# Two linear attentions in a decoder kernel: VectorE's masked copies moved behind the next level's logarithms, and sixteen small sums spread over the first products of an inverse

## Chip, cores and metric

The kernel runs on one core of a Trainium2 chip. What counts is the time of one execution in microseconds (us), as the device measures it; the median of three is given. Lower is better.

## What is computed

The reference is two blocks in a row over one sequence of 512 tokens of width 1024: two hybrid attention and retention layers, then a block of feed-forward, token mixer and feed-forward. Only the token mixer matters here. It has a pooling branch, two gated linear attentions ("hgrn" and "gla") and an RWKV-7 recurrence, all fed from one projection and joined by one output projection:

```python
p = (u @ w_in).astype(jnp.float32)
o_h = chunked_gated_linear_attention(silu(hq) * QK_SCALE, 1.0 - f, hi, log_f)      # "hgrn"
o_g = chunked_gated_linear_attention(gq * QK_SCALE, gk, gv, log_a)                 # "gla"
# both: S_t = diag(a_t) S_{t-1} + k_t^T v_t,  o_t = q_t S_t
o_r = rwkv7_scan(r_h, decay, k_h, v_h, kk, a)
# S_t = S_{t-1} diag(w_t) - (S_{t-1} kk_t)(kk_t * a_t)^T + v_t k_t^T ;  o_t = S_t r_t
bonus = jnp.sum(r_h * k_h * rwkv_r_k, axis=-1, keepdims=True) * v_h
y = jnp.concatenate([y_pool, y_hgrn, (gn(o_r) + bonus) * g_r, y_gla], axis=-1)
return y @ w_out
```

## The kernel before

Everything is float32. A weight matrix comes from memory in units of 128x1024 numbers. ScalarE rounds a unit to its high part (`sb_w_high`), VectorE takes the rest (`sb_w_low<-sb_raw,sb_w_high`), and TensorE makes a product of 128x512 in three passes for each of eight slices, so one unit is 24 matmuls ("a projection" below). There are three slots for split units and four for raw ones; the function `use()` on ScalarE and VectorE splits the unit three places ahead. Every engine runs its own hand-written list in order, and semaphores tie them together. A PSUM bank is taken by TensorE in turn (`take`, eight banks, those in `held` left out), and TensorE waits there until the engine that empties the bank has done so.

A linear attention (`linear_attention`, one function on each of the three engines) goes through nine levels, `ORDER = (32, 16, 8, 4, 2, 1, 64, 128, 256)`. For level n VectorE takes differences of summed logarithms (`sb_E<-sb_c_hgrn` or `sb_c_gla`, signal "log factor"), ScalarE raises them (`sb_E<-sb_E`, "exp factor"), VectorE multiplies by keys and queries (`sb_E<-sb_E,sb_kq_...`, "factors"), TensorE multiplies left by right halves ("pairs", line 789), and for levels up to 64 VectorE copies the result under a mask into `sb_near` (COPY_PREDICATED, line 1513, "pairs taken"). The buffer of the factors is double (`E2`), so the logarithms of level n+1 wait until TensorE has read level n-1 ("factors read"). Between the levels stands other work, by `fill(n)` on all three engines: `values` units, projections of the next branch, and in gla the eight tiles of the RWKV projection. VectorE lands such a tile in `sb_shifted` ("rwkv landed"), ScalarE makes `sb_mixed` of it ("rwkv own"), and VectorE adds the neighbour's share ("rwkv mixed"); before, both VectorE instructions stand together. Ahead of the levels are the "near" products (`bank<-sb_kq_hgrn`), whose four banks in hgrn were last those of the pooling outputs, emptied by ScalarE (`sb_y_pool<-bank`).

After gla's sixth level `operand_steps` prepares the RWKV operands: tanh and squares on ScalarE, small products on TensorE, a key norm (VectorE "key floored", GpSimd's power, ScalarE "key spread"), running sums, exponentials. `keep_busy(n)` gives TensorE n matmuls that nobody reads. Then `inverse` makes, for each of four heads, two triangular products AT and X (64 rows) and turns the operands of one tile with 128x128 transposes; VectorE masks the products, ScalarE lands the transposes. The "bonus" is 16 sums of two columns each, which ScalarE takes to `sb_small`, and GpSimd reads late in `inverse`.

## Time and profile before

| | before |
|---|---|
| median of 3 runs | 1789.72 us (1788.41 to 1791.04) |
| the profiled execution: its time, its span | 1789.85 us, 1788.0 us |
| busy: TensorE, VectorE, ScalarE, GpSimd | 96%, 49%, 38%, 7% of the span |
| mixer, up to the inverse's first products | about 969 to 1220 us |
| mean granted TensorE clock | 0.976 of full |

The span is what the profiler saw between the first and last instruction; 1.85 us lie around it. Times inside the profile count from the span's start. "Busy" of TensorE includes modelled pipeline ends. PEclk in a view of stretches is the granted clock: 1.00 is 2.4 GHz and 0.50 is 1.2 GHz. In a timeline row the first number is the start, the second the length, and brackets give the idle time before it with what ended it.

### The profile page before, as it was taken

To read this page: it belongs to the slowest core of one execution; us is meant where nothing else is said; L and a number is where in the kernel's file an instruction comes from. 1 tells how busy PE (TensorE), PEld (TensorE's weight loads), DVE (VectorE), ACT (ScalarE), POOL (GpSimd) and SP (SyncE) were. 2 spreads that over 40 slices of the span, in tenths; PEclk is the share of its full clock that TensorE was granted. 3 is DMA by queue.
4 is the path that set the end of the run, shared out by engine and by line. 5 is a ranking of instruction groups with operands and counts; after the bars stand their busy time and mean duration, and the time that the engine had idled before them with its cause. 6 is when DMAs were issued, how large, how long until landed. Compare 5 with 4: busy or idle time off the path is not lost.

```text
span 1788.0 us, 22298 instructions
## 1 busy us (share of the span) xinstructions
PE 1719.0 (96%) x8770; PEld 1397.2 (78%) x8770; DVE 876.0 (49%) x1169; ACT 674.9 (38%) x1017; POOL 128.8 (7%) x126
## 2 busy tenths in 40 slices
PE   7999999999999899999999999979998899999997
PEld 6777778878778788888888777858986688888886
DVE  5633445632445565444334775665345654444333
ACT  5145664225555333333223543363131433333221
POOL 0001002001000100000003100001320200000000
PEclk9999999999999999999999999977999999999998
DMA  5322213322222132333333211100001223323331
GB/s 193 122 71 71 83 49 105 122 81 82 77 66 81 53 112 97 96 104 89 98 97 130 71 60 59 51 27 1 1 19 48 83 83 100 101 95 96 93 98 56
DMA packets 40745, 143.92 MB, mean 80 GB/s; under 512 B 4816, under 2 KB 4832, under 8 KB 40384
## 3 DMA queue, kind: packets, MB, share of 16 engines
q1 hardware_dynamic: 37008, 130.87, 22.9%
q0 software_dynamic: 2192, 8.73, 1.5%
q10 hardware_dynamic: 1440, 2.88, 0.5%
q8 instruction: 70, 1.15, 0.3%
q14 instruction: 35, 0.29, 0.1%
HBM read 140.37 MB, written 2.10 MB: 80 GB/s over the span
## 4 chain that ended last, share of the span: by engine, by line
PE 79%; DVE 14%; ACT 6%; issue 1%; DMA 0%; DVEq 0%; ACTq 0%; SPq 0%
PE bank L450 22%; PE bank L452 21%; PE bank L451 21%; PE bank L432 8%; DVE sb_w_low L1126 3%; DVE sb_E L1126 2%; PE bank L438 2%; DVE sb_near L1513 1%; PE bank L668 1%; PE bank L647 1%; ACT sb_E L1844 1%; PE bank L604 1%; ACT sb_w_high L1844 1%; DVE sb_xg_low L1134 1%; DVE sb_x L1126 1%
## 5 line engine op out<-in xcount | busy, mean ns | idle before, releaser
L1126 DVE TENSOR_TENSOR sb_w_low<-sb_raw,sb_w_high 128x1024 fp32r<-128x1024 f32 (+1 forms) x253 | 310.5, 1227 | 390.4 <-ACT sb_w_high L1844 384.5
L450 PE MATMUL bank<-sb_xg_high,sb_w_high 128*128 128x512 f32 x1176 | 469.6, 399 | 25.1 <-DVE sb_xg_low L1134 15.3
L452 PE MATMUL bank<-sb_xg_high,sb_w_low 128*128 128x512 f32 x1176 | 462.0, 393 | 0.0
L451 PE MATMUL bank<-sb_xg_low,sb_w_high 128*128 128x512 f32 x1176 | 461.7, 393 | 0.0
L1844 ACT ACTIVATE sb_w_high<-sb_raw 128x1024 fp32r<-128x1024 f32 (+1 forms) x253 | 263.2, 1040 | 355.7 <-PE bank L452 325.2
L450 PEld LDWEIGHTS bank<-sb_xg_high,sb_w_high 128*128 128x128 f32 x1176 | 223.1, 190 | 92.6 <-issue 32.7
L452 PEld LDWEIGHTS bank<-sb_xg_high,sb_w_low 128*128 128x128 f32 x1176 | 223.0, 190 | 47.7
L451 PEld LDWEIGHTS bank<-sb_xg_low,sb_w_high 128*128 128x128 f32 x1176 | 223.4, 190 | 44.8
L452 PE MATMUL bank<-sb_h_high,sb_w_low 128*128 128x512 f32 x352 | 136.9, 389 | 0.0
L450 PE MATMUL bank<-sb_h_high,sb_w_high 128*128 128x512 f32 x352 | 136.9, 389 | 0.0
L451 PE MATMUL bank<-sb_h_low,sb_w_high 128*128 128x512 f32 x352 | 136.9, 389 | 0.0
L2413 POOL TENSOR_TENSOR sb_square_sum<-sb_square_sum,sb_square 128x512 f32<-128x512 f32 x34 | 44.7, 1315 | 957.7 <-ACT sb_square L1844 882.0
L450 PE MATMUL bank<-sb_w_high,sb_xg_high 128*128 128x512 f32 x256 | 103.4, 404 | 0.2 <-DVE sb_w_low L1126 0.2
L451 PE MATMUL bank<-sb_w_low,sb_xg_high 128*128 128x512 f32 x256 | 100.3, 392 | 0.0
L452 PE MATMUL bank<-sb_w_high,sb_xg_low 128*128 128x512 f32 x256 | 100.0, 390 | 0.0
L450 PEld LDWEIGHTS bank<-sb_h_high,sb_w_high 128*128 128x128 f32 x352 | 66.1, 188 | 13.8
L451 PEld LDWEIGHTS bank<-sb_h_low,sb_w_high 128*128 128x128 f32 x352 | 66.1, 188 | 13.7
L452 PEld LDWEIGHTS bank<-sb_h_high,sb_w_low 128*128 128x128 f32 x352 | 66.1, 188 | 13.6
L1844 ACT ACTIVATE sb_h_high<-sb_up 128x512 fp32r<-128x512 f32 x44 | 27.8, 632 | 118.7 <-DVE sb_up L1126 118.7
L1126 DVE TENSOR_TENSOR sb_up<-bank,sb_inv_rms 128x512 f32<-128x512 f32 x44 | 30.4, 691 | 81.5 <-PE bank L452 80.8
L1844 ACT ACTIVATE sb_gate<-sb_gate 128x512 f32<-128x512 f32 x44 | 27.8, 632 | 94.8 <-DVE sb_gate L1126 94.8
L450 PEld LDWEIGHTS bank<-sb_w_high,sb_xg_high 128*128 128x128 f32 x256 | 48.3, 189 | 18.3 <-issue 7.8
(336 smaller groups left out, 2109.0 us busy)
## 6 DMA issues: line engine op xcount, KB each, us to landing
sb_raw<-w_ffn_in SPq DMA_DIRECT2D x88, 512.0 KB, 3.3
sb_raw<-w_ffn_out SPq DMA_DIRECT2D x32, 512.0 KB, 3.5
sb_raw<-w_tok SPq DMA_DIRECT2D x24, 512.0 KB, 3.9
sb_raw<-w_mix_f SPq DMA_DIRECT2D x18, 512.0 KB, 3.2
sb_raw<-w_rot SPq DMA_DIRECT2D x16, 512.0 KB, 3.6
sb_raw<-w_qk SPq DMA_DIRECT2D x16, 512.0 KB, 3.3
sb_raw<-w_out SPq DMA_DIRECT2D x16, 512.0 KB, 3.3
sb_raw<-w_ffn_out SPq DMA_DIRECT2D x16, 384.0 KB, 3.1
```

The costliest lines, as they stand in the source:

```text
L432: made = e.matmul(out, lhsT, rhs, start=n == 0, stop=n == len(pairs) - 1)
L438: made = e.transpose(banks[i][:, blk(n)], in_, mem.ident)
L450: e.matmul(out, w[0], v[0], start=first, stop=False)
L451: e.matmul(out, w[0], v[1], start=False, stop=False)
L452: return e.matmul(out, w[1], v[0], start=False, stop=last)
L604: made = e.matmul(out[k], m.feat["rk"][r, f, blk(j)], m.feat["rq"][r, f, j * P:], start=part == 0, stop=part == 1)
L647: e.matmul(out[k], m.qT[r, j, blk(q)], m.kT[r, j, 0:keys], start=True, stop=True).then_inc(*p.up("scores", n, 2 * j + k, q))
L668: made = e.matmul(out[64 * k:64 * k + 64, blk(q)], m.tok["av"][:, key, h * ATT_DIM:(h + 1) * ATT_DIM], m.probT[:, 2 * (q % 2) + k, blk(key ...
L1126: e.tensor_tensor(out, a, b, op).then_inc(*v.up(*signal))
L1134: e.scalar_tensor_tensor(out=out, in0=a, scalar=scalar, in1=b, op0=op0, op1=op1).then_inc(*v.up(*signal))
L1844: e.activation(out, in_, func, bias=bias, scale=scale, accum_out=accum).then_inc(*a.up(*signal))
L2413: e.tensor_tensor(out, a, b, op).then_inc(*g.up(*signal))
```

## The change

VectorE's list changes most. The old `factor(n)` is cut in `logs(n)` and `factors(n)`. The masked copies of level n-1 stand between the two of level n+1; before, the copies of level n stood behind `fill(n+1)`. The logarithms of level 0 now stand before `fill(0)` and the near masks. In gla the mixing of a landed RWKV tile is cut off its landing and stands at the start of the next step (`mix`), except for tiles 2 and 5, which share a step with another. ScalarE does `factor(0)` before `fill(0)`. The bonus sums leave `operand_steps`; TensorE makes them in four pieces, two instructions each, behind the AT and X products of heads 0 and 1, and the turns of each tile come one head later. ScalarE's copy of the bonus stands behind the last landed transpose, and GpSimd waits for it.

```diff
-            yield
-            i = take(("bonus",), ("bonus",))
-            p.wait_ge(*of("rE"))
-            for t in range(TT):
-                for f in range(2):
...
+        bonus = take(("bonus",), ("bonus",))
+        held.add(bonus)
         for h in HEADS:
             gram("AT", h, m.bI, m.kkE)
+            if h < 2:
+                bonus_sums(2 * h)
             gram("X", h, m.kkE, m.bI)
-            turn_operands(h)
+            if h < 2:
+                bonus_sums(2 * h + 1)
+            if h:
+                turn_operands(h - 1)
+        turn_operands(3)
...
-            fill(0)
-            for h in HEADS:
-                v.wait_ge(*of("near product", name, h))
...
+                elif name == "gla":
+                    v.wait_ge(*of("factors read", "hgrn", len(ORDER) - 1 - n))
...
+            logs(0)
+            fill(0)
+            factors(0)
+            for h in HEADS:
+                v.wait_ge(*of("near product", name, h))
...
-            factor(0)
+
             for n in range(len(ORDER)):
+                mix(n)
                 if n + 1 < len(ORDER):
-                    factor(n + 1)
+                    logs(n + 1)
+                if n:
+                    scores(n - 1)
+                if n + 1 < len(ORDER):
+                    factors(n + 1)
                     fill(n + 1)
-                scores(n)
             v.mark("near done", name)
             fill(len(ORDER))
+            mix(len(ORDER))
...
                 tt(shifted, bank("rwkv", f)[:, :], mem.inv_rms, ALU.mult, "rwkv landed", f)
+                yield
                 v.wait_ge(*of("rwkv own", f))
...
+        def mix_gla(n):
+            if n < 6:
+                next(projections)
...
         def linear_attention(name, fill):
             q2, k2, c2, v2 = m.operands[name]
-            fill(0)
...
             factor(0)
+            fill(0)
...
-            a.wait_ge(*of("bonus in"))
-            act(small[:, 112:128], bank("bonus")[:, 0:16], "bonus")
...
+        a.wait_ge(*of("bonus in"))
+        act(mem.small[:, 112:128], bank("bonus")[:, 0:16], "bonus")
         finish_gla()
```

ScalarE's list at the start of hgrn, before (`sb_E` and `sb_c_hgrn` are the logarithms, `sb_w_high` a weight unit, `sb_y_pool` the pooling outputs):

```order
L1844 ACTIVATE sb_c_hgrn_131<-sb_c_hgrn_131 128x1024 [waits ScalarE_step]
L1844 ACTIVATE sb_w_high_51<-sb_raw_50 128x1024 [waits hgrn_logs,weights_used,weights_0]
L1844 ACTIVATE sb_w_high_51<-sb_raw_50 128x1024 [waits weights_high,weights_used,weights_1]
L1844 ACTIVATE sb_y_pool_125<-bank,sb_small_60,sb_cols_53 64x512 [waits weights_high,pool_out,pool_shift]
L1844 ACTIVATE sb_y_pool_125<-bank,sb_small_60,sb_cols_53 64x512 [waits y_pool,pool_out] x3
L1844 ACT_TABLE_LOAD [waits y_pool]
L1844 ACTIVATE sb_E_136<-sb_E_136 128x1024 [waits log_factor]
```

The same place of ScalarE in the changed kernel:

```order
L1872 ACTIVATE sb_c_hgrn_131<-sb_c_hgrn_131 128x1024 [waits ScalarE_step]
L1872 ACT_TABLE_LOAD [waits hgrn_logs]
L1872 ACTIVATE sb_E_136<-sb_E_136 128x1024 [waits log_factor]
L1872 ACTIVATE sb_w_high_51<-sb_raw_50 128x1024 [waits exp_factor,weights_used,weights_0]
L1872 ACTIVATE sb_w_high_51<-sb_raw_50 128x1024 [waits weights_high,weights_used,weights_1]
L1872 ACTIVATE sb_y_pool_125<-bank,sb_small_60,sb_cols_53 64x512 [waits weights_high,pool_out,pool_shift]
```

The table load and the exponential of level 0, which waits for VectorE's logarithms, moved ahead of the two weight units and of the pooling outputs.

VectorE's list late in gla, before, from the landing of RWKV tile 6 to the factors of level 6 (`sb_shifted` is a landed tile, `128x128x4` and `128x256x2` the shapes of levels 3 and 4):

```order
L1126 TENSOR_TENSOR sb_shifted_148<-bank,sb_inv_rms_58 128x512
L1134 SCALAR_TENSOR_TENSOR sb_mixed_147<-sb_shifted_148,sb_cols_53,sb_mixed_147 128x511
L1513 COPY_PREDICATED sb_near_138<-sb_mixer_120,bank 128x128x4 x2
L1126 TENSOR_TENSOR sb_E_137<-sb_c_gla_134 128x512 x2
L1126 TENSOR_TENSOR sb_E_137<-sb_E_137,sb_kq_gla_133 128x1024
L1126 TENSOR_TENSOR sb_w_low_52<-sb_raw_50,sb_w_high_51 128x768
L1126 TENSOR_TENSOR sb_shifted_148<-bank,sb_inv_rms_58 128x512
L1134 SCALAR_TENSOR_TENSOR sb_mixed_147<-sb_shifted_148,sb_cols_53,sb_mixed_147 128x511
L1513 COPY_PREDICATED sb_near_138<-sb_mixer_120,bank 128x256x2 x2
L1126 TENSOR_TENSOR sb_E_136<-sb_c_gla_134 128x8x64
L1126 TENSOR_TENSOR sb_E_136<-sb_E_136,sb_kq_gla_133 128x1024
```

The same stretch of VectorE in the changed kernel:

```order
L1133 TENSOR_TENSOR sb_shifted_148<-bank,sb_inv_rms_58 128x512
L1141 SCALAR_TENSOR_TENSOR sb_mixed_147<-sb_shifted_148,sb_cols_53,sb_mixed_147 128x511
L1133 TENSOR_TENSOR sb_E_137<-sb_c_gla_134 128x512 x2
L1531 COPY_PREDICATED sb_near_138<-sb_mixer_120,bank 128x128x4 x2
L1133 TENSOR_TENSOR sb_E_137<-sb_E_137,sb_kq_gla_133 128x1024
L1133 TENSOR_TENSOR sb_w_low_52<-sb_raw_50,sb_w_high_51 128x768
L1133 TENSOR_TENSOR sb_shifted_148<-bank,sb_inv_rms_58 128x512
L1141 SCALAR_TENSOR_TENSOR sb_mixed_147<-sb_shifted_148,sb_cols_53,sb_mixed_147 128x511
L1133 TENSOR_TENSOR sb_E_136<-sb_c_gla_134 128x8x64
L1531 COPY_PREDICATED sb_near_138<-sb_mixer_120,bank 128x256x2 x2
L1133 TENSOR_TENSOR sb_E_136<-sb_E_136,sb_kq_gla_133 128x1024
```

Each pair of masked copies went from ahead of the logarithms to between the logarithms and the product that waits for the exponential.

TensorE's list at the start of the inverse, as one piece of the difference (line 432 with `sb_kkE,sb_bI` is AT, with `sb_bI,sb_kkE` is X, with `sb_mixer,sb_sigma` the bonus sums; line 438 the turns, line 750 `keep_busy`):

```order
 L750 MATMUL bank<-sb_inv_rms_58,sb_ones_55 128x512 x5
-L432 MATMUL bank<-sb_mixer_120,sb_sigma_155 128x2 x8
 L432 MATMUL bank<-sb_kkE_149,sb_bI_151 128x128 x4
+L432 MATMUL bank<-sb_mixer_120,sb_sigma_155 128x2 x2
 L432 MATMUL bank<-sb_bI_151,sb_kkE_149 128x128 x4
+L432 MATMUL bank<-sb_mixer_120,sb_sigma_155 128x2 x2
+L432 MATMUL bank<-sb_kkE_149,sb_bI_151 128x128 x4
+L432 MATMUL bank<-sb_mixer_120,sb_sigma_155 128x2 x2
+L432 MATMUL bank<-sb_bI_151,sb_kkE_149 128x128 x4
+L432 MATMUL bank<-sb_mixer_120,sb_sigma_155 128x2 x2
 L438 MATMUL bank<-sb_shared_54,sb_kkE_149 128x128 x2
```

The sums, which stood in one block, are now pairs behind the first four triangular products. A row of the order is one instruction of the program; the trace shows each of these float32 matmuls as two.

## Rows read from the trace of the kernel before

**Rows 1.** The page, chain that ended last by engine.

```profile
PE 79%; DVE 14%; ACT 6%; issue 1%; DMA 0%; DVEq 0%; ACTq 0%; SPq 0%
```

**Rows 2.** Waits of TensorE from 1000 to 1250: total us, times, longest.

```profile
PE bank L432 <- ACT sb_mixed L1844: 8.7, 2, 5.4
PE bank L789 <- DVE sb_E L1126: 4.2, 2, 3.4
PE bank L450 <- ACT sb_v_hgrn L1844: 1.7, 1, 1.7
PE bank L432 <- DVE sb_ga L1126: 0.6, 1, 0.6
```

**Rows 3.** Timeline of ScalarE at the start of hgrn.

```profile
1002.73 2.23 ACT L1844 ACTIVATE sb_w_high<-sb_raw 128x1024 fp32r<-128x1024 f32 x2
1005.08 3.37 ACT L1844 ACTIVATE sb_y_pool<-bank,sb_small,sb_cols 64x512 f32<-64x512 f32 x4
```

**Rows 4.** Timeline of TensorE there: near products, pairs of levels 0 and 1.

```profile
1006.59 3.06 PE L432 MATMUL bank<-sb_kq_hgrn 64*128 64x128 f32 x32 [1.45 <-DVE sb_c_hgrn L1146]
...
1016.15 2.00 PE L789 MATMUL bank<-sb_E 64*128 64x64 f32 x32 [0.83 <-DVE sb_E L1126]
...
1023.74 2.00 PE L789 MATMUL bank<-sb_E 64*128 64x64 f32 x32
```

**Rows 5.** Timeline of TensorE at the end of hgrn.

```profile
1081.17 4.16 PE L432 MATMUL bank<-sb_E 64*128 64x256 f32 x16 [2.93 <-ACT sb_far L1844]
...
1085.26 0.79 PE L450 MATMUL bank<-sb_w_high,sb_xg_high 128*128 128x512 f32 x1
...
1091.83 0.44 PE L432 MATMUL bank<-sb_v_hgrn,sb_near 128*128 128x64 f32 x3
```

**Rows 6.** Stretches: length, busy us (instructions) of TensorE, its weight loads, VectorE, ScalarE, GpSimd; clock, DMA share, GB/s.

```profile
1036.20:1043.00 6.80, 6.80 (x14) 3.81 (x13) 4.99 (x7) 2.02 (x3) 0.00 (x0) 0.50 0.18 68
1080.60:1087.30 6.70, 6.13 (x21) 4.63 (x22) 1.26 (x2) 4.87 (x9) 0.00 (x0) 0.50 0.25 81
...
1224.00:1244.30 20.30, 20.30 (x89) 18.56 (x89) 11.04 (x14) 8.95 (x15) 2.54 (x2) 0.50 0.00 1
```

**Rows 7.** Timeline of TensorE: last pass of RWKV tile 6.

```profile
1159.84 0.39 PE L452 MATMUL bank<-sb_xg_high,sb_w_low 128*128 128x512 f32 x1
```

**Rows 8.** Timeline of VectorE late in gla.

```profile
1165.16 0.69 DVE L1126 TENSOR_TENSOR sb_shifted<-bank,sb_inv_rms 128x512 f32<-128x512 f32 x1
1166.64 0.75 DVE L1134 SCALAR_TENSOR_TENSOR sb_mixed<-sb_shifted,sb_cols,sb_mixed 128x511 f32<-128x511 f32 x1 [0.79 <-ACT sb_mixed L1844]
1167.50 1.51 DVE L1513 COPY_PREDICATED sb_near<-sb_mixer,bank 128x512 f32<-128x512 int32 x2
1169.05 1.42 DVE L1126 TENSOR_TENSOR sb_E<-sb_c_gla 128x512 f32<-128x512 f32 x2
1171.59 1.51 DVE L1126 TENSOR_TENSOR sb_E<-sb_E,sb_kq_gla 128x1024 f32<-128x1024 f32 x1 [1.12 <-ACT sb_E L1844]
...
1176.60 2.68 DVE L1513 COPY_PREDICATED sb_near<-sb_mixer,bank 128x512 f32<-128x512 int32 x2
...
1189.53 0.17 DVE L1130 TENSOR_SCALAR sb_small<-bank 128x16 f32<-128x16 f32 x1
...
1197.08 1.23 DVE L1126 TENSOR_TENSOR sb_E<-sb_E,sb_kq_gla 128x1024 f32<-128x1024 f32 x1 [3.99 <-ACT sb_E L1844]
```

**Rows 9.** Timeline of ScalarE late in gla.

```profile
1166.63 1.28 ACT L1844 ACT_TABLE_LOAD   x1
1167.92 1.06 ACT L1844 ACTIVATE sb_v_gla<-sb_v_gla 128x1024 f32<-128x1024 f32 x1
...
1181.42 0.63 ACT L1844 ACTIVATE sb_mixed<-sb_mixed 64x512 f32<-64x512 f32 x1
...
1193.33 1.05 ACT L1844 ACTIVATE sb_kI<-sb_small 128x1024 f32<-128x1024 f32 x1
```

**Rows 10.** Timeline of TensorE: bonus sums, and AT of head 1.

```profile
1220.16 1.95 PE L432 MATMUL bank<-sb_mixer,sb_sigma 128*128 128x2 f32 x16 [0.20 <-DVE sb_rE L1126]
...
1225.97 2.07 PE L432 MATMUL bank<-sb_kkE,sb_bI 64*128 64x128 f32 x8
```

More of the change, by code:

```diff
@@ L954, in turn_operands, with bonus_sums @@
                 transposes(i, [pair[n // 2][:, n % 2, blk(t)] for n in range(4)], name + " turned", t)
+        def bonus_sums(t):
+            for f in range(2):
+                at = 4 * t + 2 * f
+                group(banks[bonus][:, at:at + 2], [(m.sigma[:, f, blk(t)], mem.table("same_head")[:, 0:P:64])],
+                      "bonus in")
+        bonus = take(("bonus",), ("bonus",))
+        held.add(bonus)
         for h in HEADS:
             gram("AT", h, m.bI, m.kkE)
+            if h < 2:
+                bonus_sums(2 * h)
             gram("X", h, m.kkE, m.bI)
-            turn_operands(h)
+            if h < 2:
[3 more added lines that the diff above has]
+        turn_operands(3)
+        held.discard(bonus)
         def side_products():
@@ L2507, in inverse @@
         g.wait_ge(*of("tokB", TT - 1))
+        g.wait_ge(*of("bonus"))
         for i in range(TT):
```

33 lines of the change are left out of this document (16 added, 17 removed).

## The prediction

> **What bounds the kernel now.** I read the chain that ended last first: TensorE has 79% of it, VectorE 14%, ScalarE 6% [rows 1]. So a change on VectorE counts only where TensorE waits for it. The change touches the mixer from about 1003 to 1246, and there the list of TensorE's waits is short: 8.7 us for ScalarE's work on `sb_mixed`, 4.2 us for factors, 1.7 us for the landed values, 0.6 us for `sb_ga` [rows 2]. Third I read the stretches in which the granted clock is 0.50, that is 1.2 GHz in place of 2.4: 6.8 us at 1036, 6.7 us at 1081 and 20.3 us from 1224 on, with TensorE busy nearly all through [rows 6]. Work that fills such a stretch would take half as long at the full clock, so these three hold 3.4, 3.4 and 10.2 us. Those are as large as the waits, and the forecast depends on both. The time line of TensorE says what went ahead of each: level 2's narrow products and waits before 1036, an idle time of 2.9 us before 1081 [rows 5], and before 1224 no idle time at all but the block of 16 two-column sums, 1.95 us, and products on 64 rows [rows 10].
>
> From level to level of hgrn TensorE starts a group of pairs every 7.6 us (1016.15 to 1023.74) [rows 4]: 2.0 for the pairs, 5.6 for 24 projection passes. This 7.6 is what VectorE must stay under.
>
> **Part 1, the front of hgrn: a loss.** In ScalarE's list the exponential of level 0 now stands ahead of two weight units and the pooling outputs. The near products need the banks that the pooling outputs leave. Before, ScalarE ran units and pooling from 1002.73 on while VectorE was still summing [rows 3], and the near products started at 1006.59, when the sums were done [rows 4]. Now: sums done 1006.45, two logarithms 1.42 [rows 8], exponential 1.06 (the length of the other 128x1024 activation, [rows 9]), to 1009.0; two units 2.23, to 1011.4; first pooling output 3.37/4 = 0.84 [rows 3], to 1012.3. TensorE starts the near products at 1012.4, 5.8 us late, after 7.3 us of idle time (it fell idle 1.45 us before 1006.59, at 1005.1). The queue behind ScalarE's waiting exponential is all of this; VectorE's two `sb_w_low` wait for the units as well, but TensorE needs them later.
>
> What the clock makes of it: the trace has the clock halved around an idle time of 2.9 us [rows 5, 6], so I take it as certain after 7.3 us. The near products take 3.06 us at full clock [rows 4] and, with a spacing of 0.21 us for such products at half clock (eight in about 1.7 of their 2.07 us, [rows 10]), 6.8 us for 32: to 1019.2. In the stretch at 1081 the clock came back about 2 us after wide products had begun (1085.26, against 1087.3) [rows 5, 6]; I take 3.3 us here, to 1022.5. In these, 1.65 of the projection's 5.6 us get done, the other 3.95 run at full clock: pairs of level 0 at 1026.45 in place of 1016.15. **+10.3.** Without any clock loss the near products would pace with the pooling outputs and end at 1015.8, and the pairs would start at 1021.4, +5.3; that is the lower bound.
>
> The Trainium skill (TensorE: Matmul & The Clock Gate, section Why this matters for your kernels) warns of idle gaps between bursts of matmuls, after which the clock is halved; that speaks against this part of the change, and the 2.9 us wait in the trace agrees.
>
> **Part 2, hgrn behind the front: the time comes back.** TensorE now arrives late, so what it waited for is there: landed values and `sb_ga`, **-2.3** [rows 2]. The half clock at 1036 followed narrow products that were broken by that wait. With the wait gone I take the full clock, **-3.4**; how sure that is, stands below. At the end, TensorE stood 2.9 us before level 8 and then ran at half clock: from 1081.17 to the next product with values at 1091.83 are 10.7 us [rows 5]. At full clock this is 1.9 (half of nearly 4) for the pairs and 5.6 for the projection, 7.5. That needs factors 8 in time. VectorE's steps in the new list: late ones have logarithms 1.42, a copy pair 2.7 [rows 8] (over the exponential), factors 1.23 and a unit as long [rows 8], with gaps 2.6, landing 0.7: 7.4, and one with `sb_c_gla` 1.3 more. From the end of pairs 5, VectorE has factors 8 after 13.4 us, and TensorE (projection, pairs 6, values, pairs 7: 5.6 + 2 + 5.6 + 1.1) wants them after 14.3. (The 13.4: logarithms 1.45, copies 2.7, factors and unit 2.6, landing 0.7, `sb_c_gla` 1.3, logarithms 1.45, copies 1.6, factors 1.25; the 1.1 and the 1.6 are estimates by size.) So there is no wait, by a small margin. **-2.9 - 3.2 = -6.1.** The unhidden exponential was the reason for the old wait: one gap of 1.12 per level [rows 8] on an engine at or over 7.6.
>
> The front's loss is thus paid back almost exactly: +10.3 - 2.3 - 3.4 - 6.1 = -1.5 when hgrn ends.
>
> **Part 3, gla: the gain.** Up to the last pass of RWKV tile 6, ending at 1160.2 [rows 7], TensorE goes without waits that matter, so no VectorE saving counts until there. But VectorE lands that tile only at 1165.16, 5 us behind [rows 8]: each step held the wait of 0.79 for ScalarE's `rwkv own`, the exponential's 1.12 and the copies in the open. In the new list the exponential is covered by the copies and, for most tiles, mixing stands later. So VectorE meets TensorE there. From then on I add up the chain: landing 0.69, own share 0.8, to 1161.7. ScalarE then bends gla's gate, a table load, 1.06, a table load, 3.9 together [rows 9], to 1165.6; exponential 1.06; factors 1.51 and gap, to 1168.3; a 768-wide unit 1.05; landing, wait and mixing 0.69 + 0.79 + 0.85, to 1171.7; one logarithm 0.7; the copies of level 4, 2.7, to 1175.1; factors 1.3; logarithms 1.45; copies of level 5, 2.7; factors 1.3, to 1181.8; and then the key norm's floor, which stood at 1189.53 [rows 8]. **-7.6.** What follows is a chain that the change doesn't touch: key spread at 1193.33 [rows 9], level 8's factors at 1197.08 after a wait of 3.99 for ScalarE [rows 8], running sums, operands, and the first sum of the inverse at 1220.16. It starts earlier as a whole. The tanh that TensorE waited 5.4 us for (in the 8.7 of [rows 2]; 1181.42 in [rows 9]) follows exponential 6 and moves to about 1174, so that wait shrinks too, on TensorE's side of the same chain. The copies of 2.7 are longer than the exponential of 1.3 that they cover; this is the price that keeps the gain at 7.6 and not more.
>
> **Part 4, the inverse.** TensorE has the same products; moving a bonus sum costs nothing there while it is only moved. VectorE's masks waited for ScalarE's presets, which stood behind the bonus copy; they come earlier, but nothing waits for them. The clock decides. Between the sums still stand only 64-row products, for some 5.5 us in all, so I expect the clock to fall as before. But turns 2 and 3 and the first full-width products now stand together at the end, where before one turn did, and it was there that the clock came back. I take 4 us less of the 20.3 at half clock, an estimate, and half of it as time: **-2.0**; bounds 0 (nothing, as the total work is the same) and -10.2 (no half clock at all).
>
> GpSimd's new wait for the bonus is hidden: it reads it after gla's output, 65 us later than the sums. The queue of weight loads is moved past nothing; two units are split 4 us later at the front, with tens of us before their successors are used.
>
> **Sum.** -1.5 - 7.6 - 2.0 = -11.1 on the profiled execution's own time, 1789.85 (span 1788.0 and 1.85 around it), which is the median of 1789.72 to within 0.13: **1778.8**.
>
> **Rivals.**
> - **A, the clock holds in the inverse.** For it: the near products on 64 rows at 1006.59, after 1.45 us idle [rows 4], didn't bring the clock down; it fell after the unbroken block of sums, which is now in pieces of half a us. Against it: a third of the first 5.5 us is still sums. The whole 20.3 us [rows 6] halve: -10.2 in place of -2.0, **1770.6**.
> - **B, another half-clock stretch in hgrn.** Level 2's pairs and the four 16-row gate products still stand together, 3.9 us without a wide product. If the clock falls there again, or level 8 waits after all, 3 to 3.4 come back, both 6.5: **1782 to 1785**.
> - **C, no help from the order of the sums.** The work of the inverse is the same and the half clock lasts 20.3 us again: **1780.8**. The Trainium skill page named above puts a fall down to idle time, and by it strewing the sums changes nothing; this trace has TensorE busy 20.30 of 20.30 us in that stretch and next to no idle time ahead of it, so the page doesn't explain the fall.
> - **D, slower.** The copies now stand between TensorE and its factors. If VectorE's step, 7.4 to 8.7 us late in hgrn, stays over TensorE's 7.6 with the delay of the front added, the debt isn't repaid, and in gla each level pays copies minus exponential (0.4, and 1.6 on levels 4 and 5) where it hoped to gain. With the gains of parts 2 (but 2.3) to 4 gone: 1789.85 + 10.3 - 2.3 = **1797.9**. It decides once less than 8 us of the later gains arrive. Against it: VectorE had 5 us of lag in gla only, and a late TensorE gives it more room.
> - **E, nothing to see.** The gains just pay the front: within 3.6 us of before.
>
> **Chances.** My forecast, 1775.5 to 1782 for itself, has 0.40; A 0.21; B 0.17; C 0.09; D 0.07; E 0.06. The range from 1769.5 to 1785 leaves out D, E and the edges of A and B. About 0.2%, 3.6 us, is what a measurement of this kernel can tell from no change. Faster by more: 0.86; within: 0.07; slower: 0.07.
>
> **What the profile after would show.** Near products at about 1012.4, behind ScalarE's pooling outputs, then a clock of 0.50 to about 1022. Pairs 0 near 1026. No wait before level 8 of hgrn, and its values products within 1 or 2 us of before. RWKV tile 6 landed within 1 us of TensorE's last pass. Key floor and first inverse product some 9 us earlier. The inverse's low stretch shorter than 20 us. I am wrong if the front's loss lasts into gla, if VectorE lands tile 6 late again, or if the clock takes other turns than these, since 3 to 10 us hang on each of them.

## The result, and the profile after

The changed kernel takes **1777.98 us** (median of 4 runs, 1776.87 to 1780.97) against 1789.92 for the kernel before in the same session: ratio 0.9948, 95% interval 0.9926 to 0.9969. By the medians it is faster by 11.9 us, by the ratio by 9.3. The profiled execution was the slowest of the four: 1780.97, with a span of 1779.2, against the 1788.0 of before. So the spans of the two traces differ by 8.8 us.

The chain of work that ended last, by engine, to be held against [rows 1]:

```profile
PE 84%; DVE 10%; ACT 4%; issue 1%; DMA 0%; POOL 0%; DVEq 0%; ACTq 0%; SPq 0%
```

VectorE went from 14% to 10% and ScalarE from 6% to 4%. TensorE's waits from 1000 to 1250, to be held against [rows 2] (total us, times, longest):

```profile
PE bank L432 <- ACT sb_y_pool L1872: 7.0, 1, 7.0
PE bank L432 <- ACT sb_mixed L1872: 5.0, 2, 2.9
PE bank L432 <- ACT sb_Pm L1872: 1.4, 1, 1.4
PE bank L432 <- DVE sb_bI L1141: 1.3, 1, 1.3
```

The waits for `sb_E`, `sb_v_hgrn` and `sb_ga`, 6.5 us in all, are gone, and so is the one of 2.93 us before level 8 [rows 5]; the one for `sb_mixed` is 3.7 us smaller. New are 7.0 us for the pooling outputs. The waits for `sb_Pm` (0.4 us before) and `sb_bI` (0.2 before) grew.

ScalarE's timeline at the start of hgrn, to be held against [rows 3]:

```profile
1007.84 1.06 ACT L1872 ACTIVATE sb_E<-sb_E 128x1024 f32<-128x1024 f32 x1 [3.95 <-DVE sb_E L1133]
1009.01 2.23 ACT L1872 ACTIVATE sb_w_high<-sb_raw 128x1024 fp32r<-128x1024 f32 x2
1011.35 3.38 ACT L1872 ACTIVATE sb_y_pool<-bank,sb_small,sb_cols 64x512 f32<-64x512 f32 x4
```

TensorE there, and at the end of hgrn, to be held against [rows 4, 5]:

```profile
1003.28 1.93 PE L432 MATMUL bank<-sb_window,sb_pool_w 64*64 64x512 f32 x8
1012.18 5.13 PE L432 MATMUL bank<-sb_kq_hgrn 64*128 64x128 f32 x32 [6.97 <-ACT sb_y_pool L1872]
...
1024.61 2.00 PE L789 MATMUL bank<-sb_E 64*128 64x64 f32 x32
...
1079.80 3.74 PE L432 MATMUL bank<-sb_E 64*128 64x128 f32 x32
...
1089.08 1.22 PE L432 MATMUL bank<-sb_v_hgrn,sb_near 128*128 128x64 f32 x10
```

ScalarE waits 3.95 us for the logarithms with 5.6 us of work queued behind the wait, and TensorE waits for that work. The pairs of level 0 start 8.5 us later than before (1024.61 against 1016.15). At 1079.80 the two last groups of pairs run as one row, without the wait of 2.93 between them, and the products with values start at 1089.08, 2.75 us earlier than before.

The stretches, at the front of hgrn, at the two places of hgrn shown in [rows 6], and in the inverse (columns as there):

```profile
1007.30:1020.90 13.60, 8.72 (x41) 7.73 (x42) 8.62 (x11) 7.53 (x9) 0.00 (x0) 0.50 0.25 78
1036.20:1043.00 6.80, 6.80 (x52) 5.24 (x51) 5.22 (x7) 1.66 (x2) 0.00 (x0) 1.00 0.25 77
1080.60:1087.30 6.70, 6.69 (x41) 5.37 (x39) 1.82 (x2) 4.93 (x9) 0.00 (x0) 1.00 0.23 81
1212.10:1232.50 20.40, 20.40 (x89) 18.81 (x89) 9.33 (x12) 3.91 (x7) 1.85 (x2) 0.50 0.00 0
```

The clock is halved for 13.6 us at the front and no longer at 1036 and 1081: from 1021 to 1170 its mean is 1.00. In the inverse it is halved for as long as before. (On the far right of a row stand DMA share and GB/s.)

Late in gla there are more half-clock stretches, which the prediction doesn't list: 13.6 and some 6.8 us before, 3.4 and 6.7 us after. The longest of before, and the second of after:

```profile
1172.70:1186.30 13.60, 7.79 (x42) 5.15 (x43) 10.73 (x12) 4.05 (x6) 0.00 (x0) 0.50 0.10 29
```

```profile
1178.00:1184.70 6.70, 4.59 (x18) 3.61 (x17) 3.27 (x6) 4.90 (x7) 3.44 (x1) 0.50 0.01 2
```

TensorE is busy for only 7.79 of the 13.60 us and 4.59 of the 6.70; the rest it waits. No run tells what the clock costs there.

VectorE late in gla, to be held against [rows 8]:

```profile
1156.71 0.69 DVE L1133 TENSOR_TENSOR sb_shifted<-bank,sb_inv_rms 128x512 f32<-128x512 f32 x1 [0.48 <-PE bank L452]
...
1168.77 2.63 DVE L1531 COPY_PREDICATED sb_near<-sb_mixer,bank 128x512 f32<-128x512 int32 x2
1171.51 1.23 DVE L1133 TENSOR_TENSOR sb_E<-sb_E,sb_kq_gla 128x1024 f32<-128x1024 f32 x1
...
1178.36 0.17 DVE L1137 TENSOR_SCALAR sb_small<-bank 128x16 f32<-128x16 f32 x1
```

RWKV tile 6 is landed at 1156.71, behind a wait for TensorE: VectorE has caught up, where before it was 5 us behind. The factors follow the copies without idle time, because the exponential lies under them. The key norm's floor stands at 1178.36, 11.2 us earlier than in [rows 8].

The start of the inverse on TensorE, then ScalarE's end of that block, and the same end in the kernel before:

```profile
1208.98 1.16 PE L432 MATMUL bank<-sb_kkE,sb_bI 64*128 64x128 f32 x8 [0.20 <-DVE sb_rE L1133]
...
1236.03 1.11 PE L432 MATMUL bank<-sb_Pm,sb_XT 128*128 128x64 f32 x8 [1.39 <-ACT sb_Pm L1872]
```

```profile
1232.88 0.60 ACT L1872 ACTIVATE sb_tokB<-bank 128x512 f32<-128x512 f32 x1
1233.51 0.19 ACT L1872 ACTIVATE sb_small<-bank 128x16 f32<-128x16 f32 x1
1233.77 1.28 ACT L1872 ACT_TABLE_LOAD   x1
1235.07 0.22 ACT L1872 ACTIVATE sb_small<-sb_small 128x16 f32<-128x16 f32 x1
1235.38 1.29 ACT L1872 ACTIVATE sb_Pm<-bank 128x512 f32<-128x512 f32 x2
```

```profile
1242.91 0.60 ACT L1844 ACTIVATE sb_tokB<-bank 128x512 f32<-128x512 f32 x1 [0.26 <-PE bank L438]
1243.59 1.28 ACT L1844 ACT_TABLE_LOAD   x1
...
1245.19 1.29 ACT L1844 ACTIVATE sb_Pm<-bank 128x512 f32<-128x512 f32 x2
```

ScalarE's last turned operand, the bonus, a table load and gla's root end only at 1235.3, and `sb_Pm` stands behind them. Before, ScalarE still had to wait 0.26 us for its last turned operand; after, the turns of two tiles come together and the last one queues. From the first product of the inverse to the first of `sb_Pm` with `sb_XT` it takes 27.05 us; before it took 25.68 (1220.16 to 1245.84). The table load costs 1.28 us here, and the root follows it 1.30 us after its start. The Trainium skill (ScalarE: Activation LUTs, section What ACT_TABLE_LOAD costs) gives the same 1283 ns for the load, but 2.66 us for a switch with the drain of the engine; no such drain shows in this row.

### The profile page after: what moved, and what is told of

It is laid out like the page before. It is cut to its first block, busy times and chain, and to the rows that moved or that the text cites. A ratio compares the mean times of both kernels' runs of the same rounds, so it can differ in the third digit from the quotient of the medians.

```text
span 1779.2 us, 22284 instructions
## 1 busy us (share of the span) xinstructions
PE 1716.0 (96%) x8770; PEld 1396.2 (78%) x8770; DVE 875.6 (49%) x1169; ACT 675.5 (38%) x1017; POOL 129.3 (7%) x126
## 4 chain that ended last, share of the span: by engine, by line
PE 84%; DVE 10%; ACT 4%; issue 1%; DMA 0%; POOL 0%; DVEq 0%; ACTq 0%; SPq 0%
PE bank L450 23%; PE bank L451 22%; PE bank L452 22%; PE bank L432 8%; PE bank L438 2%; DVE sb_w_low L1133 2%; PE bank L789 1%; DVE sb_rot L1133 1%; PE bank L668 1%; PE bank L647 1%; PE bank L604 1%; DVE sb_xg_low L1141 1%; ACT sb_w_high L1872 1%; DVE sb_x L1133 1%; PE bank L527 0%
```

## The experiments

To compare traces that arrive at the mixer at different moments, I count us from the start of TensorE's first pooling product (1003.21 before, 1003.28 after). All numbers in this table are of one profiled execution of each kernel, the ratio is that of the runs to the kernel before.

| kernel | first near product | pairs 0 | hgrn values | inverse | Pm with XT | inverse to Pm | ratio, 95% interval |
|---|---|---|---|---|---|---|---|
| before | 3.38 | 12.9 | 88.6 | 217.0 | 242.6 | 25.7 | 1 |
| after | 8.90 | 21.3 | 85.8 | 205.7 | 232.8 | 27.0 | 0.9948 (0.9926 to 0.9969) |
| after_again | 8.90 | 21.9 | 86.4 | 206.3 | 232.9 | 26.7 | 0.9957 (0.9943 to 0.9971) |
| e_front_only | 9.06 | 21.5 | 94.0 | 220.3 | 247.3 | 27.0 | 1.0033 (1.0020 to 1.0046) |
| e_front_act | 3.41 | 15.2 | 79.7 | 199.6 | 226.2 | 26.6 | 0.9920 (0.9905 to 0.9935) |
| e_copies_back | 9.07 | 21.9 | 93.1 | 216.2 | 242.7 | 26.5 | 1.0012 (1.0003 to 1.0022) |
| e_mix_back | 9.02 | 20.6 | 86.6 | 206.7 | 233.4 | 26.6 | 0.9968 (0.9954 to 0.9983) |
| e_bonus_back | 8.87 | 19.0 | 83.5 | 203.3 | 228.9 | 25.6 | 0.9958 (0.9943 to 0.9973) |
| e_bonus_only | 3.22 | 12.8 | 88.3 | 216.9 | 241.9 | 25.0 | 1.0016 (1.0000 to 1.0031) |
| e_busy_front | 15.74 | 24.2 | 91.7 | 211.6 | 237.2 | 25.6 | 0.9975 (0.9963 to 0.9987) |
| e_busy_inverse | 9.02 | 21.4 | 87.4 | 207.3 | 233.1 | 25.8 | 0.9980 (0.9967 to 0.9993) |
| e_norm_front | 3.18 | 11.9 | 76.7 | 196.6 | 222.1 | 25.5 | 0.9905 (0.9887 to 0.9924) |
| e_pads | 3.33 | 12.0 | 78.4 | 198.3 | 216.7 | 18.4 | 0.9876 (0.9857 to 0.9894) |
| e_pads_front | 3.72 | 12.2 | 78.4 | 198.3 | 216.7 | 18.4 | 0.9874 (0.9855 to 0.9893) |

Some of the expectations count from the last pooling product's row, 1.34 us later than this table does.

**The same kernel again.** The measure for the three kernels that end this section:

> The changed kernel itself once more, unaltered, as the measure for the other three of this group. Both theories: 0.993 to 0.997 of the kernel before, half clock of 13.7 us at the front of hgrn and 20.5 us in the inverse as in the first profile. If the half-clock stretches differ from execution to execution by a step or more at these places, single traces are worth less than their sums suggest.

Measured: 1778.27 us, 11 runs from 1773.65 to 1781.84, beside 1787.52 for the kernel before, ratio 0.9957. The two long half-clock stretches came again, 13.7 and 20.5 us. Between the two traces of this one kernel the spans differ by 7.4 us (1779.2 and 1771.8); they reach the mixer 2.1 us apart, and from Pm with XT to the end one took 543.2 us and the other 537.7. Two stretches at about the same place behind the inverse, in the first trace and in the second:

```profile
1341.80:1345.10 3.30, 3.30 (x9) 2.73 (x10) 1.39 (x2) 2.03 (x4) 0.00 (x0) 0.50 0.00 0
1406.70:1410.00 3.30, 3.30 (x9) 2.61 (x8) 2.29 (x2) 1.76 (x2) 0.00 (x0) 0.50 0.08 12
```

```profile
1341.00:1345.00 4.00, 4.00 (x22) 3.03 (x21) 1.48 (x3) 1.41 (x3) 0.00 (x0) 1.00 0.34 106
1406.60:1410.00 3.40, 3.40 (x17) 2.82 (x16) 0.94 (x1) 1.06 (x1) 0.00 (x0) 1.00 0.55 161
```

At the full clock TensorE has 16 to 22 instructions in such a stretch, at half of it 9. So the clock outside the change moves the time of one and the same kernel by some us from execution to execution, and a difference under 2 us can be read only locally, in the trace.

**The front alone, on the kernel before.** On VectorE and ScalarE, in both hgrn and gla:

```diff
 # VectorE
-            fill(0)
...
             def factor(n):
...
+                if n == 0:
+                    fill(0)
                 v.wait_ge(*of("exp factor", name, n))
                 tt(exps, exps, k_and_q, ALU.mult, "factors", name, n)
+                if n == 0:
+                    near_part()
 # ScalarE
-            fill(0)
...
             factor(0)
+            fill(0)
```

> The kernel before with the change's new front alone: in hgrn and gla the logarithms and the exponential of level 0 stand ahead of the units and pooling outputs; copies, mixing and bonus sums as before. Theory (a stall that is paid back): near products 5.6 us later (1012.2), pairs of level 0 about 8.5 us later (1024.6), but the waits for landed values and sb_ga (2.3), the half-clock stretch at 1036 (3.4) and the 2.9 us wait with its half clock before level 8 (6.1) shrink or go, so hgrn's products with values start within 2 us of 1091.83, and the time is 1788 to 1792. Rival (a stall adds): values at about 1100, time 1798.

Measured: slower, 1.0033 (1.0020 to 1.0046), that is +5.9 us. Pairs of level 0 stand at +8.5, values of hgrn at +5.4, the inverse at +3.3. So 3.1 of the 8.5 us come back in hgrn and another 2.0 in gla, and the theory that hgrn pays the stall back falls. TensorE's waits in the mixer, and the end of hgrn:

```profile
PE bank L432 <- ACT sb_mixed L1850: 10.1, 2, 6.9
PE bank L432 <- ACT sb_y_pool L1850: 7.1, 1, 7.1
PE bank L432 <- ACT sb_far L1850: 4.4, 2, 3.8
```

```profile
1087.02 4.16 PE L432 MATMUL bank<-sb_E 64*128 64x256 f32 x16 [3.80 <-ACT sb_far L1850]
```

The waits for `sb_v_hgrn` and `sb_ga` are gone as expected (2.3 us), and of the 6.8 us at half clock at 1036 a stretch of 3.4 is left, at 1045, which is 1.7 us of time. But the wait before level 8 grew from 2.93 to 3.80, and with it the half clock stayed there: 2.3 + 1.7 - 0.9 is the 3.1. A late TensorE doesn't shorten VectorE's step: the idle exponential is still in each. In the inverse this trace has 23.9 us of half clock where the kernel before has 20.5, and its 27.0 us to Pm with XT go with that. Whether the 2.0 us in gla come from TensorE's lateness or from gla's own new front, no run separates.

**The new lists, with ScalarE's old front.** On the changed kernel, in hgrn alone; VectorE's front stays new:

```diff
 # ScalarE, linear_attention
-            factor(0)
-            fill(0)
+            if name == "hgrn":
+                fill(0)
+                factor(0)
+            else:
+                factor(0)
+                fill(0)
```

> The changed kernel, with ScalarE's old order at the front of hgrn alone (units and pooling outputs ahead of the exponential of level 0). Theory (the stall was mostly paid back): near products at about 1006.6 and pairs of level 0 at 1016 again, but the waits of 2.3 and the half clock at 1036 return, so that of 8.5 us only 2 to 4 arrive: 1774 to 1776. Rival (additive): all 8.5 arrive, 1769.5. Second rival (VectorE sets the end of hgrn in any case): nothing arrives, 1778.

Measured: 0.9920, some 6 us faster than the changed kernel (by ratio 0.28 and 0.37% under its two, 5.0 and 6.6 us). The near products start 5.5 us earlier and the values of hgrn 6.1; this is kept to the inverse (6.1). That is near the additive rival and over what I expected. In this trace the clock fell at the front even so, for 6.8 us:

```profile
1006.80:1013.50 6.70, 6.70 (x22) 5.41 (x21) 5.79 (x8) 2.19 (x2) 0.00 (x0) 0.50 0.47 158
```

In `e_norm_front` and `e_pads`, whose front is the same, it didn't, and their pairs 0 stand at 11.9 and 12.0. The values of hgrn stand at 79.7 to 76.7, 9 to 12 us earlier than before, with a front that is not late at all. The waits for landed values and `sb_ga` (2.3 us of [rows 2]) are nearly gone here too (0.2 us in two of these kernels, none in this), and none is left before level 8. So the new list doesn't need the delay to be rid of them. The delay alone removes the 2.3 us as well, but not the wait before level 8, which needs VectorE's new list.

**The copies behind the factors again.** On the changed kernel:

```diff
 # VectorE, linear_attention
                 if n + 1 < len(ORDER):
                     logs(n + 1)
-                if n:
-                    scores(n - 1)
-                if n + 1 < len(ORDER):
                     factors(n + 1)
                     fill(n + 1)
+                scores(n)
```

> The changed kernel, with VectorE's masked copies again behind the factors of the next level and its unit, so that the exponential lies open again; new front, split mixing and strewn sums stay. Theory (the copies' place is what gained in hgrn, not the late TensorE): hgrn's products with values start about 8 us later than in the changed kernel, as with the new front alone (92.6 us behind the last pooling output where the changed kernel has 84.5), and the key norm is late again; time 1788 to 1792. Rival (the debt of the front is repaid by lateness, whatever VectorE does): values at 84.5 to 87, time 1778 to 1783.

Measured: 1.0012; everything that the change gained is gone. The values of hgrn stand 7.3 us later than in the changed kernel, the inverse 10.5. VectorE late in gla:

```profile
1186.60 1.22 DVE L1133 TENSOR_TENSOR sb_E<-sb_E,sb_kq_gla 128x1024 f32<-128x1024 f32 x1 [1.36 <-ACT sb_E L1870]
1187.93 0.18 DVE L1137 TENSOR_SCALAR sb_small<-bank 128x16 f32<-128x16 f32 x1
```

The idle time for the exponential is back (1.36), and the key norm's floor is 10.1 us later than after, counted from the pooling product.

With this, four combinations of VectorE's list and ScalarE's front can be compared at hgrn's values, which neither mixing nor bonus sums reach. A kernel whose only differences lie behind hgrn counts as the same combination, and the spread within one is wide:

| hgrn's values | ScalarE's old front | the new front |
|---|---|---|
| VectorE's copies as before | 88.6, 88.3 | 94.0, 93.1 |
| VectorE's copies moved | 79.7, 76.7, 78.4 | 85.8, 86.4, 86.6, 83.5, 87.4 |

The new front costs about 5 us with the old list and about 8 with the new. The new list gives about 10 us with the old front and 7.5 with the new. Traces of one combination differ by up to 4 us, so it stays open whether the two simply add. With neither list is the front's cost gone when hgrn ends.

**Mixing at once again.** On the changed kernel:

```diff
 # VectorE, rwkv_steps
                 tt(shifted, bank("rwkv", f)[:, :], mem.inv_rms, ALU.mult, "rwkv landed", f)
-                yield
                 v.wait_ge(*of("rwkv own", f))
...
 # VectorE, fill_gla and mix_gla
                 if n in (2, 4):
                     next(projections)
-                    next(projections)
...
         def mix_gla(n):
-            if n < 6:
-                next(projections)
+            pass
```

> The changed kernel with each landed RWKV tile mixed at once again, behind a wait for ScalarE's own share, in place of one step later. Theory (the split pays only where VectorE is behind, late in gla): hgrn as in the changed kernel, tile 6 landed 1 to 4 us later, first product of the inverse 1 to 4 us later, time 1779 to 1782. Rival (the split is worth nothing, the hidden exponential did it all): 1778. Second rival (the split was most of gla's 9 us): 1784 or more.

Measured: 0.9968 against 0.9948 and 0.9957 of the changed kernel, 2 to 3.6 us, with intervals that overlap. In the trace the inverse stands at 206.7 against 205.7 and 206.3, but 0.2 to 0.8 us of that are already there at hgrn's values, ahead of everything that this edit changes. What is left of the 2 to 3.6 us of the runs the trace does not show. The traces of five kernels say more, from hgrn's values to the inverse, and around RWKV tile 6 (us):

| kernel | copies moved | mixing later | tile 6: last pass to landing | last pass to key floor | hgrn values to inverse |
|---|---|---|---|---|---|
| before | no | no | 4.9 | 29.3 | 128.3 |
| e_front_only | no | no | 3.5 | 27.9 | 126.3 |
| e_copies_back | no | yes | 0.9 | 24.5 | 123.1 |
| e_mix_back | yes | no | 0.3 | 21.9 | 120.1 |
| after | yes | yes | 0.0 | 21.7 | 119.9 |

So in gla the two edits do part of the same work: each alone lets VectorE nearly catch up at tile 6. Beside the moved copies the later mixing is worth 0.2 us, and without them 3.2. The copies' place is worth 3.2 us beside the later mixing and 6.2 without it. This is one trace for each row, but from hgrn's values to the inverse all nine traces of kernels with both edits lie between 119.85 and 119.90.

**The bonus sums in one block again.** On the changed kernel, and the reverse edit alone on the kernel before. The sums, ScalarE's copy of them and the turns move together:

```diff
 # TensorE, inverse
-        bonus = take(("bonus",), ("bonus",))
-        held.add(bonus)
         for h in HEADS:
             gram("AT", h, m.bI, m.kkE)
-            if h < 2:
-                bonus_sums(2 * h)
             gram("X", h, m.kkE, m.bI)
-            if h < 2:
-                bonus_sums(2 * h + 1)
-            if h:
-                turn_operands(h - 1)
-        turn_operands(3)
-        held.discard(bonus)
+            turn_operands(h)
```

> The changed kernel with the sums for the bonus in one block ahead of the inverse again and each turn of operands behind its own head. Theory (the shifted turns crowd ScalarE's end of the block): first product of sb_Pm with sb_XT 25.7 us after the first product of that stretch, where the changed kernel has 27.05; a half-clock stretch of 20.5 us as before; time 1.4 less, 1776.6. Rival (strewing gains by the clock, as forecast): 2 us more, 1780, with a longer half-clock stretch than the changed kernel's 20.5.

> The kernel before with only the strewn bonus sums and the turns shifted by a head. Theory: the same 20.5 us of half clock, ScalarE's turned operands, bonus, table load and root end later than the first product for sb_Pm, TensorE waits about 1.4 us for sb_Pm where it waited 0.4; time 1 to 1.5 more, 1791. Rival (clock comes back sooner): 16 us of half clock, time 2 less, 1788. Timing alone will hardly tell these apart, the trace should.

Measured: 0.9958 without the strewing, the same as the changed kernel's 0.9957. In its trace the half-clock stretch is 20.5 us again, and 25.6 us pass to Pm with XT where the changed kernel took 27.0 and 26.7: 1.1 to 1.4 us better in the trace. With the strewing alone the runs give 1.0016, hardly told from 1. There the trace speaks for the rival in part: the half clock lasted 17.1 us, not 20.5, and the way took 25.0 us, 0.6 less than before; but TensorE waited 0.9 us for `sb_Pm`, where it waited 0.4. In the changed kernel, run twice, strewing didn't shorten the half clock. Over all traces without added products in the inverse, strewn sums have 20.5 us six times and 17.1 twice, sums in one block 20.5 twice and 23.9 once. That isn't enough to say that strewing shortens it. What stands is the wait: 1.4 and 1.0 us for `sb_Pm` with the turns shifted in the changed kernel, 0.3 without.

**The idle time at the front filled.** On the changed kernel:

```diff
 # TensorE, pool_outputs
                     group(banks[i][r, :], [(m.pool_w[r, f, :], m.window[r, f, :])], "pool out", f, r.start)
+            for _ in range(16):
+                e.matmul(banks[i][0:64, :], mem.ones[:, 0:64], mem.inv_rms, start=True, stop=True)
```

> The changed kernel with 16 products of 512 columns and 128 rows, read by nobody, behind hgrn's pooling outputs on TensorE, into rows of the last pooling bank that are unused: they fill the 7 us in which it waits for ScalarE. They add no time to the path. Theory (of the front's 8.5 us about 5.6 are idle time and 3 the halved clock): no clock of 0.50 between 1003 and 1022, near products at 1012 as before, pairs of level 0 at 1021.4 in place of 1024.6, time 3 us less, 1775. Rival (the near products on 64 rows bring the clock down by themselves): a low stretch stays, behind the start of the near products, and the pairs start within 1.5 us of 1024.6.

Measured: 0.9975, and a size of mine was off: 16 such products take 13.95 us (two rows in the trace for each), so they did add time and the near products started 6.8 us later than after:

```profile
1004.66 13.95 PE L770 MATMUL bank<-sb_inv_rms,sb_ones 128*64 128x512 f32 x32
1018.53 2.82 PE L432 MATMUL bank<-sb_kq_hgrn 64*128 64x128 f32 x32
```

```profile
1003.00:1022.00 19.00, 19.00 (x75) 7.84 (x72) 10.08 (x11) 6.82 (x8) 0.00 (x0) 1.00 0.17 55
```

But it answers the question on the clock. With the gap filled no half clock is left at the front, and from the first near product to the pairs of level 0 pass 8.42 us (to 1026.95), where the changed kernel took 12.43 at half clock and the kernel before 9.56. So of the front's +8.5 us at the pairs, 5.5 are the later start and the other 2.9 are time behind it, the halved clock's: 4.0 against a front without any gap. This much of the theory holds. That the padding costs nothing doesn't.

**Wide products among the triangles.** On the changed kernel:

```diff
 # TensorE, inverse
+        def unread():
+            e.matmul(banks[bonus][:, 16:512], mem.ones, mem.inv_rms[:, 16:512], start=True, stop=True)
+
         for h in HEADS:
             gram("AT", h, m.bI, m.kkE)
+            unread()
...
             gram("X", h, m.kkE, m.bI)
+            unread()
```

> The changed kernel with one product of 496 columns and 128 rows, read by nobody, behind each of the 8 triangle groups at the start of the inverse, into unused columns of the bonus bank: 3.3 us more work for TensorE at full clock. Theory (the clock falls for narrow products on 64 rows, with no idle time needed): the half-clock stretch of 20.5 us goes or is cut by more than half, and from the first product of the inverse to the first of sb_Pm with sb_XT pass 19 to 24 us where 27.0 did; time 1771 to 1776. Rival (products do not hold the clock): the stretch stays at 20 us or grows, and the added products cost 3.3 to 6.6 us: 1781 to 1785.

Measured: the half clock of the inverse is gone, all of it:

```profile
1210.40:1236.10 25.70, 23.61 (x144) 17.79 (x144) 11.66 (x16) 8.31 (x14) 5.06 (x4) 1.00 0.00 1
```

But the way to Pm with XT is 25.8 us, only 0.8 to 1.2 less than after: eight products cost 7.5 us (0.94 each from start to start, again over twice my figure), and the wait for `sb_Pm` grew to 2.1. The theory is right on the clock and wrong on the price. The runs are even 0.23% above the changed kernel's second measurement (0.9980 against 0.9957), 4 us that this trace, whose span of 1779.1 is within the changed kernel's two, doesn't show; they stay open.

**Three kernels built on this.** `e_norm_front` takes ScalarE's old front, and moves gla's squares, sum and root into idle time at the start of the inverse:

```diff
 # VectorE, inverse
             first_pairs("X", m.X[:, h, :], h, mem.table("pairs_ts"), "X made", 2, h)
-        finish_gla()
+            if h < 2:
+                finish_gla(1 - h)
 # finish_gla(1): squares and their sum; finish_gla(0): from the wait for the root on
 # ScalarE, inverse
         fence("inverse")
+        finish_gla()
         for i in range(TT):
...
         act(mem.small[:, 112:128], bank("bonus")[:, 0:16], "bonus")
-        finish_gla()
```

`e_pads` adds to it one unread product for each of the two first heads, and `e_pads_front` adds to that two at the front of hgrn:

```diff
 # e_pads: TensorE, inverse
             gram("AT", h, m.bI, m.kkE)
             if h < 2:
+                e.matmul(banks[bonus][:, 16:512], mem.ones, mem.inv_rms[:, 16:512], start=True, stop=True)
                 bonus_sums(2 * h)
 # e_pads_front: TensorE, pool_outputs
+            for _ in range(2):
+                e.matmul(banks[i][0:64, :], mem.ones[:, 0:64], mem.inv_rms, start=True, stop=True)
```

> The changed kernel with ScalarE's old order at the front of hgrn, and with gla's squares, their sum and root moved ahead of the turned operands into idle time of VectorE and ScalarE in the inverse, where they stood behind them. Theory (table load and root, 1.6 us, stood between ScalarE's last turned operand and Pm): no TensorE wait for sb_Pm of over 0.4 us (0.9 with the old front alone), 25.6 us or less from the first product of the inverse to the first of sb_Pm with sb_XT, and 1 us less than with the old front alone: ratio 0.991. Rival (the wait is only moved, to VectorE's X or GpSimd's masks): 26.6 us again, 0.992.

> The kernel e_norm_front with two products of 496 columns and 128 rows that nobody reads, one behind the AT triangle of head 0 and one of head 1, where no turned operand follows yet: 1.7 us more work. Theory (the clock falls in those first narrow heads alone, and heads 2 and 3 with their full-row turns hold it): no half clock between 1195 and 1235, first product of the inverse to first of sb_Pm with sb_XT in 17.5 to 19 us, time 6 to 8 us below e_norm_front, ratio 0.987. Rival (only constant padding holds it, as with 8 products): the stretch returns later and at least 17 us long; 1 to 3 us above e_norm_front, 0.992 to 0.993.

> The kernel e_pads with two more unread products of 512 columns behind hgrn's pooling outputs, 1.7 us, in TensorE's idle time of 1.5 to 2 us there. Theory (near products and that gap bring the clock down at the front): no clock of 0.50 between 1000 and 1020, pairs of level 0 within 9.6 us of the first near product where the old front alone took 11.7, time 2 us below e_pads. Rival (padding there doesn't cover the near products on 64 rows): low stretch as before, at or up to 1 us over e_pads.

Measured: `e_norm_front` 0.9905, 25.5 us to Pm with XT, 1.1 less than with the old front alone, and no wait for `sb_Pm` left in TensorE's list. Its ScalarE:

```profile
1204.47 1.28 ACT L1881 ACT_TABLE_LOAD   x1 [5.02 <-DVE sb_small L1149]
1205.77 0.22 ACT L1881 ACTIVATE sb_small<-sb_small 128x16 f32<-128x16 f32 x1
1208.18 0.60 ACT L1881 ACTIVATE sb_tokA<-bank 128x512 f32<-128x512 f32 x1 [2.20 <-PE bank L438]
...
1222.89 0.60 ACT L1881 ACTIVATE sb_Pm<-bank 128x512 f32<-128x512 f32 x1
```

Load and root lie in 9 us of idle time. `e_pads` has 0.9876, 1763.24 us: the way takes 18.4 us in place of 25.5, 7.1 less, at the price of two products of 0.94 us. Stretches of `e_norm_front` and of `e_pads`, from the second head or the start of the inverse on:

```profile
1201.50:1221.80 20.30, 20.30 (x89) 18.73 (x90) 11.93 (x15) 5.68 (x9) 1.53 (x2) 0.50 0.01 1
```

```profile
1201.20:1217.20 16.00, 16.00 (x116) 13.78 (x117) 12.44 (x16) 6.36 (x11) 2.56 (x2) 1.00 0.00 1
1195.00:1235.00 40.00, 39.42 (x285) 33.65 (x285) 25.14 (x36) 15.47 (x26) 8.27 (x7) 1.00 0.00 1
```

Padding of the two heads without turns is enough; heads 2 and 3, unpadded, ran at the full clock. The three traces with such products added in the inverse have no half clock there, and the eleven without have 17.1 to 23.9 us of it. `e_pads_front` is the same within error (0.9874): with or without its padding the clock held at the front in these three traces, and it gave nothing. `e_pads` and `e_pads_front` beat the kernel before and the changed one, with intervals that lie wholly below the latter's.

## Why the prediction came out, and where it didn't

The forecast was 1778.8, the measurement 1777.98. The sum came out, but that is in part luck: part 4 was wrong in sign, and part 2 gives a wrong reason for a good number.

- **Part 1, +10.3: right in mechanism, 1.8 too large.** Near products were forecast for 1012.4 and stand at 1012.18, behind exponential, units and pooling as described, and the clock is halved to 1020.9 (forecast 1022.5). The near products took 5.1 us at it and not 6.8. Measured +8.5.
- **Part 2, -2.3 - 3.4 - 6.1, "the time comes back": the number came, the cause was wrong in half of its terms.** Measured at hgrn's values is -2.75 in all, against the forecast -1.5. But the front alone gets back only 3.1 of its 8.5 us in hgrn, and the new list without the late front gives 8.9 to 11.9 us there. Most of what I wrote as the return of a debt is the gain of hiding the exponential under the copies. It was there to be had without the debt: with the new list the front cost 6.1 us at hgrn's values and still 6.1 at the inverse. The step that failed is "the time comes back", with "TensorE now arrives late, so what it waited for is there". Lateness by itself gave 2.3 us of waits and 1.7 of the 3.4 us of clock, and cost 0.9 before level 8; the new list gives the same without it. A step-by-step sum along one path can't tell such causes apart; only the runs of the combinations could. The part that spoke of VectorE's step (exponential covered, factors of level 8 in time) is the one that holds, though the items in its sum of 13.4 us add up to 13.05.
- **Part 3, -7.6: right.** From hgrn's values to the inverse the trace has 119.9 us where it had 128.3, -8.4. VectorE meets TensorE at tile 6 as foreseen, and from that tile's last pass to the key norm's floor 21.7 us pass, where the forecast's chain has 21.6 and the trace before 29.3. The other 0.8 us lie ahead of it, with the wait of 0.7 us for `sb_v_gla` gone. The copies' place and the later mixing do the same work in part: 3.2 us for the one and 0.2 for the other as the last edit, 6.2 and 3.2 as the only one.
- **Part 4, -2.0: wrong in sign.** The half clock lasted 20.5 us as before, so the strewing gave nothing (rival C, for this part), and the shifted turns brought a wait that I hadn't priced: two turns now end together on ScalarE, ahead of bonus, table load, root and `sb_Pm`. +1.4. The copy of the bonus, 0.19 us in that queue, isn't separated from the turns by any run. That ScalarE's queue was moved, too, was in the difference and not in my sum.
- The end: 542.2 us from Pm with XT on before, 543.2 after, +1.0. Both traces have 10.2 us at half clock there, ahead of the last 15 us, so what makes this 1.0 stays open; it is less than the 5.4 between the two traces of the changed kernel.

By terms: +8.5 - 11.2 (part 2, to the -2.75) - 8.4 + 1.4 + 1.0, which is the -8.8 between the spans but for rounding. The forecast had -11.1, the medians have -11.9 and the ratio -9.3; the profiled execution was 3 us slower than the median of its kernel, which by the spread of after_again (8 us) is nothing out of the way.

Rivals: A's gain, the clock held in the inverse, exists and is worth 7 us net, but needs two wide products, not strewn sums. B didn't come in the changed kernel, though single traces of its variants show a half clock of 3.4 us in hgrn (at 1045 in `e_front_only`, at 1043 in `e_mix_back`) or of 6.8 (at 1046 in `e_busy_front`). D's mechanism, the copies between TensorE and its factors, didn't show: the factors followed them in time.

## What to carry to other kernels

- Where one engine waits for a function of another's on every step, put independent work of its own between the request and the wait. It should be about as long as the function. Here 2.6 us of copies, put where 1.1 to 1.4 us had been idle at each level, took some 8 to 10 us out of hgrn, and 3 or 6 us out of gla, with or without the later mixing.
- Moving one instruction ahead in a queue moves everything behind it, with its waits. Here an exponential that had to wait 3.95 us for its input was put ahead of 5.6 us of ready work that another engine needed. VectorE needed the new order and ScalarE didn't; ScalarE's old one was worth 6 us.
- When a forecast lets a delay "pay for itself", test the delay alone and the rest alone before believing it.

## What the runs showed of the hardware

- TensorE's clock fell to 0.50 in the inverse with TensorE busy in all of the stretch (20.40 of 20.40 us) and a wait of 0.20 us ahead of it. The work was products on 64 rows, turns of 128x128 and sums of 2 columns. With two products of 496 columns on 128 rows, 1.9 us of work for nobody, it stayed at 1.00 for that whole stretch, in `e_pads` and in `e_pads_front`. The Trainium skill (TensorE: Matmul & The Clock Gate, section Why this matters for your kernels) warns of idle gaps. At the front of hgrn the trace agrees (7 us idle, 13.6 us at half clock, and none when the gap was filled), but it doesn't account for the inverse.
- One program's execution can hold or lose the clock at the same place: with an equal front the near products and what follows to the pairs of level 0 took 11.8 us in `e_front_act` and 8.7 in `e_norm_front`.
- VectorE's multiplication of `sb_y_gla` by the broadcast norms, 128x1024, took 2.00 us in the changed kernel at 1235.60 and 1.23 us in `e_norm_front` at 1207.40. GpSimd ran a 1.27 us operation on `sb_CT` from 1235.25, beside the first; beside the second it was idle. The other traces agree: where GpSimd had started first, VectorE's instruction grew to 1.56 (before), 1.60 (`e_bonus_back`, `e_front_only`), 1.96 (`e_busy_front`) and 2.00 us, in each case by about 0.15 us less than the overlap. In the second trace of the changed kernel VectorE started 0.07 us ahead, at 1233.66: it took 1.23 us, and GpSimd's operation 2.27 in place of 1.27. So the one that starts second is held up; no run was made to try this by itself.
